# Input projection: every second half-chunk of the weights requested from GpSimd's queue

## The reference, cut to what matters

```python
def _project(x, attn_norm, w_in):
    h = _rmsnorm(x, attn_norm)
    proj = jnp.einsum('bsd,de->bse', h, w_in)        # d = 1024, e = 4096
    q_sb, k_sb, v_sb, z_sb, q_dl, k_dl, v_dl, z_dl = jnp.split(proj, 8, axis=-1)
```

## Time and profile before

| | us |
|---|---|
| median of three executions | 3229.28 (3226.84 to 3233.21) |
| the profiled execution | 3229.47, span 3227.9 |
| TensorE busy | 2910.8 (90% of the span) |
| VectorE busy | 1674.2 (52%) |
| ScalarE busy | 1496.1 (46%) |
| GpSimd busy | 648.6 (20%) |
| half 0 of the projection | 1.0 to 409.1 |
| half 1 of the projection | from 410.3 |

### The profile page before, as it was taken

One profiled execution on the slowest core, in us unless ns is written; L12 is line 12 of the kernel. 1 busy time (PEld: TensorE's weight loads), 2 busy tenths in 40 slices (PEclk: granted clock), 3 DMA queues, 4 the chain that ended last, 5 costly groups with the idle time before them and its releaser, 6 DMA issues. The chain is left out here.

```text
span 3227.9 us, 47243 instructions
## 1 busy us (share of the span) xinstructions
PE 2910.8 (90%) x17678; PEld 2098.9 (65%) x17678; DVE 1674.2 (52%) x2736; ACT 1496.1 (46%) x2618; POOL 648.6 (20%) x959
## 2 busy tenths in 40 slices
PE   7999969999799999998999968888888773799998
PEld 5888848888555555554888855555555441588887
DVE  2000042322578888887666635555555434666663
ACT  4122142222477777776666624555555423333332
POOL 0000011212122222221033333344443200000000
PEclk9999989999899999999999979999999986899999
DMA  5444444445401010101233229999999886432321
GB/s 175 171 150 173 166 155 156 164 154 190 132 1 40 1 40 1 38 9 53 74 103 80 76 67 421 420 420 420 421 421 420 369 319 224 139 104 104 104 84 41
DMA packets 193925, 548.62 MB, mean 170 GB/s; under 512 B 30240, under 2 KB 99456, under 8 KB 157888
## 3 DMA queue, kind: packets, MB, share of 16 engines
q0 software_dynamic: 45568, 348.22, 27.5%
q1 hardware_dynamic: 148160, 197.75, 18.4%
HBM read 486.21 MB, written 126.68 MB: 190 GB/s over the span
## 5 line engine op out<-in xcount | busy, mean ns | idle before, releaser
L1464 DVE COPY sbs_kT<-sbs_ps_T 128x512 f32<-128x512 f32 x256 | 270.8, 1093 | 268.9 <-PE sbs_ps_T L1626 268.8
L418 PE MATMUL proj_ps_G<-proj_w_hi,proj_xT_hi 128*128 128x512 f32 x1024 | 402.4, 393 | 4.0 <-DVE proj_xT_lo L290 4.0
L422 PE MATMUL proj_ps_G<-proj_w_hi,proj_xT_lo 128*128 128x512 f32 x1024 | 399.5, 390 | 0.0
L420 PE MATMUL proj_ps_G<-proj_w_lo,proj_xT_hi 128*128 128x512 f32 x1024 | 399.4, 390 | 0.0
L362 ACT ACTIVATE proj_out<-proj_ps_G,proj_stat 128x512 f32<-128x512 f32 (+1 forms) x136 | 93.3, 688 | 567.3 <-PE proj_ps_G L422 562.6
L1626 PE MATMUL sbs_ps_T<-held,sbs_k_ring 128*128 128x128 f32 x2048 | 279.5, 292 | 43.0 <-ACT sbs_kT L1547 39.1
L290 DVE TENSOR_TENSOR proj_xT_lo<-proj_ps_T,proj_xT_hi 128x512 fp32r<-128x512 f32 (+1 forms) x68 | 42.2, 662 | 508.4 <-ACT proj_xT_hi L352 508.4
L1626 PEld LDWEIGHTS sbs_ps_T<-held,sbs_k_ring 128*128 128x128 f32 x2048 | 248.2, 153 | 86.3 <-ACT sbs_kT L1547 42.3
L626 POOL CAST sbp_sp_hi<-sbp_sp 128x512 fp32r<-128x512 f32 (+3 forms) x320 | 171.8, 551 | 505.8 <-DVE sbp_sp L668 499.8
L1547 ACT ACTIVATE sbs_kT<-sbs_ps_T 128x512 f32<-128x512 f32 x256 | 260.2, 1115 | 4.9 <-PE sbs_ps_T L1626 4.4
L668 DVE SCALAR_TENSOR_TENSOR sbp_sp<-sbp_Z,sbp_el 128x512 f32<-128x512 f32 (+3 forms) x320 | 179.9, 603 | 118.8 <-ACT sbp_el L746 118.5
(11 more groups left out here) (289 smaller groups left out, 5880.3 us busy)
## 6 DMA issues: line engine op xcount, KB each, us to landing
out_k_win_s<-in_cache_k_win POOLq DMA_DIRECT2D x16, 2044.0 KB, 8.5
out_v_win_s<-in_cache_v_win POOLq DMA_DIRECT2D x16, 2044.0 KB, 8.1
proj_out<-in_w_in SPq DMA_DIRECT2D x32, 512.0 KB, 5.3
proj_x_in<-in_x_prompt SPq DMA_DIRECT2D x32, 512.0 KB, 3.8
dls_k_in<-in_cache_k_win SPq DMA_DIRECT2D x16, 1024.0 KB, 10.2
dls_v_in<-in_cache_v_win SPq DMA_DIRECT2D x16, 1024.0 KB, 14.2
merge_o<-scratch_o_dil SPq DMA_DIRECT2D x48, 256.0 KB, 4.7
merge_x<-in_x_prompt SPq DMA_DIRECT2D x16, 512.0 KB, 4.5
```

What stands on the lines that cost most here:

```text
L418: nc.tensor.matmul(ps_G[0:n, g, :], xT_hi[:, slot, k, 0:n], w_hi[:, k, cols], start=(k == 0), stop=False)
L420: nc.tensor.matmul(ps_G[0:n, g, :], xT_hi[:, slot, k, 0:n], w_lo[:, k, cols], start=False, stop=False)
L422: mm = nc.tensor.matmul(ps_G[0:n, g, :], xT_lo[:, slot, k, 0:n], w_hi[:, k, cols], start=False, stop=(k == KC - 1))
L1464: nc.vector.tensor_copy(by_lane(kT[:, j, :, :])[:, :, i, :], ps_T[:, x % TB, :].rearrange("p (a n) -> p a n", a=PAIRS)).then_inc(kT_odd, 1)
```

## The change

SyncE keeps the even half-chunks, GpSimd requests the odd ones: c1 and c3 as its first two instructions, ahead of the memset, and c5 to c15 after `rms(0)` and ahead of its items. Each waits for the same count of `w_split` as before and lands in the same room with the same semaphore. High parts, splits and matmuls are unchanged.

```diff
+        def load_weights(eng, c):
+            eng.dma_start(stage[:, c % 4, :], w_rows[:, c // 2, C0 + (c % 2) * D:C0 + (c % 2 + 1) * D]) \
+                .then_inc(w_loaded[c % 4], 16)
+
         @block.sync
         def _(sp):
...
             sp.dma_start(x_in[0:NS, 0, :], x_s).then_inc(x_loaded[0], 16)
-            for c in range(2 * KC):
+            for c in range(0, 2 * KC, 2):
                 if c >= 4:
                     hold(sp, w_split, c - 3)
-                sp.dma_start(stage[:, c % 4, :], w_rows[:, c // 2, C0 + (c % 2) * D:C0 + (c % 2 + 1) * D]) \
-                    .then_inc(w_loaded[c % 4], 16)
+                load_weights(sp, c)
...
         @block.gpsimd
         def _(pool):
+            load_weights(pool, 1)
+            load_weights(pool, 3)
             nc.gpsimd.memset(mhalf[:, :], -0.5).then_inc(mhalf_set, 1)
             hold(pool, mhalf_set, 1)
...
             rms(0, 0, 0)
+            for c in range(5, 2 * KC, 2):
+                hold(pool, w_split, c - 3)
+                load_weights(pool, c)
             steps(pool, body)
```

## The result

| | before | changed |
|---|---|---|
| median, us | 3229.28 | 3243.8 (3241.1 to 3247.93) |
| the profiled execution, us | 3229.47 | 3241.73, span 3239.7 |
| ratio to before | | 1.0049, 95% interval 1.0036 to 1.0061 |

The change costs 14.5 us by the medians, 12.3 us by the two profiled executions. I had forecast 3233.2 us and a range to 3241.0: the side was right, the size was not.

A forecast was written before the change was run, and what follows sets the result against it. Weight loads, not SyncE's requests, were taken to bound the starts of the halves. Start 1.4, GpSimd order 0.7, later rounds 1.2 and tail 0.6 summed to 3.9 us, giving 3233.2 us, range 3225.0 to 3241.0 us.

The forecast's parts named there:

- What bounds the kernel: Starts of both halves: weight loads set the pace, 1.9 us per half-chunk; SyncE's requesting does not, so moving requests saves nothing.
- c1 and c3 at the start: Start of each half: the early 1 MB delays c0 by 1.2 us in the first half, 0.2 in the second.
- The tail: End of item 0: item 1's x_in load competes with c15, 0.3 us per half, 0.6 in all.
- The order in GpSimd's queue: c5 stands behind rms(0), asked for 1 us late; it costs 0.5 and 0.2 us, 0.7 in all.
- the rounds: Later rounds of the rooms: four further GpSimd loads each add half of e = 0.6 us, 1.2 us in all.
- (A): Rival: no cost, no gain, as rounds absorb e and c1, c3 fit in idle engine time; 3229.5 us, chance 0.25.
- (B): Rival: faster, two queues keep the engines better fed and loads land in 3.8 us; 3222.5 us, chance 0.10.
- (C): Rival: slower, GpSimd kept from preparing requests while VectorE splits, e becomes 1.9 us; 3242.4 us, chance 0.12.
- (D): Rival: after item 0 a moving pause can add or remove a dip of TensorE's clock, 1.7 us either way; decides none.
- The signs I had named: Profile after: c0's high part at 8.3 us, c5's request about 13, last splits 2.6 and 1.3 us later.
- my 0.6: Price e of GpSimd's queue: each load lands 0.6 us later after issue than from SyncE, bounds 0.2 and 1.5.
- my sum: Main case, all terms of the change added: 3.9 us slower, 3233.2 us, chance 0.45.

The follow-up runs named there:

- the first experiment: Of the change only its start: c1 and c3 requested first from GpSimd, all else from SyncE as in the kernel before; ratio to before 1.0015.
- the first two experiments: Only the change's start (c1 and c3 early from GpSimd), ratio to before 1.0015; and the change without that start, c0 to c3 from SyncE, 1.0018.

## Why the prediction was wrong

**What bounds the kernel: right.** The loads set the pace and SyncE's requests did not; a second queue had nothing to give, from GpSimd (0.9999 with it, 0.9992 without, rows behind c15 in both) or from ScalarE (0.9986 with it, 0.9985 without). This is what the Trainium skill, DMA: Bandwidth & Descriptors, section "Rules for kernel authors", states as a rule, and the runs agree. Its other half, that the issuing engine's time is saved, was worth nothing.

**c1 and c3 at the start: this step failed.** I set 1.2 + 0.2 = 1.4 us, with bounds of 2 and 1; measured are 2.9 + 2.9 = 5.8 us, outside both. The working took the megabyte as engine time, 2.8 us, and let it fill whatever time was free. In the first half nothing like the 0.8 us of free time was of use: c0 was asked for as early as before and landed 2.9 us later. In the second I had counted 3.1 us of idle engines as room enough, and had left the moment of c0's request where it was. But what lay in that room were thousands of small packets of the constants, and beside GpSimd's queue of 4 KB packets these went one for one, 81 against 81, so that the table of rotations landed 2.8 us later. SyncE, held in its request for `x_sample`, asked for c0 2.85 us late. A free share of an engine's time is not room if somebody's short packets have to take turns with long ones in it, and if the next request stands behind them.

The Trainium skill, DMA: Bandwidth & Descriptors, section "Queues, rings and completion order", says that an engine goes round the queues that have work, packet by packet, and that a packet typically holds 9 to 17 descriptors. The turns are there in this trace. They are shorter than that, though: one small row, and within 6 ns the start of one 4 KB row, not batches of either.

**The tail: a term mis-sized.** 0.3 us per half, with a bound of 1.3; measured 1.6 and 1.0. That the rows' load would hold up c15 was the right mechanism. I let the sharing with c14 pay most of it back, and nothing did: the rows landed first, and moving them behind c15 gave 2.7 and 1.5 us.

**The order in GpSimd's queue and the rounds: about right.** 0.7 + 1.2 = 1.9 us, measured 1.5 from c4's request to c15's. The sum is no proof of its parts: in the four kernels in which SyncE makes all twelve requests and no constants are moved, they take from 19.5 to 20.7 us in the first half and from 20.0 to 21.2 in the second. c5 was asked for 1.0 us late, as I had said, though only 0.44 of it is `rms(0)`; a lone load from GpSimd cost 0.4 us more and not 0.6.

**The rivals.** (A) assumed the start free; it is excluded by the first experiment. (B) had nothing in it: from request to landing the changed kernel has 5.7 us in the median against 5.3. (C), GpSimd kept waiting by VectorE, would have shown as requests past 1 us; they last 530 ns in the median and 761 at most, and the request for c7 goes 0.3 us after its split's end. The time came near to (C)'s 3242.4 us by another road, which a time alone could not have told. (D), the clock, was real: the slow stretch at the end of item 0 of the first half is there in the changed kernel and in the first two experiments, where the rest of that half takes 373.04 to 373.11 us, and in none of the others, where it takes 371.42 to 371.49. It costs 1.6 us each time.

**The signs I had named.** c0's high part came at 9.99 us, not at 8.3; the request for c5 at 14.7, not 13; the last splits 5.5 and 4.4 us late, not 2.6 and 1.3. GpSimd's loads landed in 6.0 us in the median and SyncE's in 5.4, which looks like my 0.6, but the two sets are different half-chunks, and with all 32 from GpSimd the median is 5.3.

**The range.** With the start's 5.8 and the tail's 2.6 in the place of 1.4 and 0.6, my sum becomes 3.9 + 4.4 + 2.0 = 10.3 us, and 11.9 with the clock, against 12.3 of the profiled pair. The start's 5.8 us are nearly twice its upper bound of 3, and the tail's 2.6 are all of its own (twice 1.3), so a range that stopped at 3241.0 could not hold the two together with the clock. What the medians have beyond the profiled pair, 2 us, is within the spread of single runs.

## What to carry to other kernels

A request made early is not free because its data is needed later and its engine is idle: it is served ahead of, or in turn with, whatever the first step waits for. It can even delay the request of what is needed first, when that stands in another queue behind small pieces. A wrong order at the start cost 6 us here, and a second queue brought nothing that could be measured. Before moving a load to another queue, list what shares the DMA engines with it at both ends of the loop, the small constants at the start and the next stage's first load at the end, and ask which of these the critical path waits for. Then make requests in the order of need. Small constants that are used late can go behind the first loads of data: here that brought the second half's first step forward by 2.35 us and its last split by 1.5.

## What the runs showed beside it

- Two queues that both have work take turns row by row, whatever the rows' lengths, so long rows are unfair to short ones: the rotation table (64-byte rows) took 6.4 us to land beside 1 MB of 4 KB rows in another queue, 3.6 us without it, and 9.9 us beside 2 MB.
- A request can last long by itself: SyncE's for `x_sample`, behind the constants of the second half, took 2.02 us before and 4.87 us in the changed kernel, where 0.3 to 0.6 us are usual, and all later requests of that engine wait for it.
- A load that shares GpSimd's queue with a 2 MB copy from memory to memory lands in 9.2 us (item 4's) instead of 4.0.
- GpSimd has its request going about 0.3 us after the split that it waits for, SyncE within 0.1 us; in a loop bound by loads of 5.3 us this was not to be seen in the time.
- A pause of TensorE is followed in some executions by a stretch at the lower clock level and in others not: at the end of item 0 of the first half it fell after pauses of 3.4, 2.1 and 2.4 us, and stayed up after 2.8 us in the kernel before. Where it fell it cost 1.6 us, which is a tenth of the effect measured here and would be all of a smaller one.
